# First four output blocks on the unscaled input, with the norm's factor applied at their eviction

## The reference

```python
def rms_norm(x, g):
    y = xf * lax.rsqrt(jnp.mean(xf * xf, axis=-1, keepdims=True) + RMS_EPS)
    return (y * g.astype(jnp.float32)).astype(x.dtype)
...
h = rms_norm(x, g_mix_pre)
proj = jnp.einsum('btd,dc->btc', h, w_in)
q_r, f_r, i_r, g_r, q_a, k_a, v_a = jnp.split(proj, splits, axis=-1)
...
z = heads(f_in)
f = lbh + (1.0 - lbh) * jax.nn.sigmoid(z)
```

## Time and profile before

| | |
|---|---|
| median of 3 runs | 1590.98 us |
| profiled execution | 1592.15 us, span 1590.4 |
| PE busy | 1536.7 us, 97% |
| DVE busy | 997.5 us, 63% |
| ACT busy | 850.3 us, 53% |
| POOL busy | 129.9 us, 8% |
| mean granted clock of PE | 0.993 |
| moved from and to HBM | 156 GB/s over the span |

### The profile page before, as it was taken

The page is one execution under the profiler, slowest core; times in us unless marked ns, Lnnn a source line. Parts: engine busy times, 40 slices in busy tenths (PEclk is TensorE's granted clock), DMA queues, the critical chain, the costliest instruction groups (busy, mean ns, idle before and its releaser), DMA issues.

```text
span 1590.4 us, 29827 instructions
## 1 busy us (share of the span) xinstructions
PE 1536.7 (97%) x11984; PEld 1463.5 (92%) x11984; DVE 997.5 (63%) x1675; ACT 850.3 (53%) x1540; POOL 129.9 (8%) x165
## 2 busy tenths in 40 slices
PE   5999999899999999999999999998999999999996
PEld 5998789898999999999999987898899999999996
DVE  6683778774548655345887656878645675553466
ACT  6445655476455755234664565445755465551552
POOL 4120123000000000000002100330000000000000
PEclk9999999999999999999999999999999999999998
DMA  6644664353454555334443467343534545552453
GB/s 202 202 137 164 235 217 133 107 179 107 134 165 153 167 190 180 114 107 150 155 146 120 141 219 266 121 141 115 169 104 148 164 154 179 182 183 80 133 154 118
DMA packets 83237, 247.89 MB, mean 156 GB/s; under 512 B 8691, under 2 KB 26483, under 8 KB 82972
## 3 DMA queue, kind: packets, MB, share of 16 engines
q1 hardware_dynamic: 83100, 245.98, 48.2%
HBM read 234.13 MB, written 14.44 MB: 156 GB/s over the span
## 4 chain that ended last, share of the span: by engine, by line
PE 86%; DVE 8%; ACT 2%; issue 2%; DMA 1%; SPq 0%; DVEq 0%; ACTq 0%
PE ps L1030 68%; PE ps L1027 7%; PE ps L1083 3%; DVE w_rest L1347 2%; PE ps L1233 1%; PE ps L1220 1%; PE ps L1248 1%; DVE reg L1385 1%; DMA kc<-kcT 1%; DVE x L1389 1%; DVE norm_every L1370 1%; DVE square_sum L1360 1%; ACT w_high L749 1%; PE ps L1058 1%; PE ps L1206 0%
## 5 line engine op out<-in xcount | busy, mean ns | idle before, releaser
L1030 PE MATMUL ps<-h_high,w_rest 128*128 128x320 f32 (+1 forms) x1920 | 581.2, 303 | 8.5 <-DVE h_rest L1409 5.8
L1030 PE MATMUL ps<-h_rest,w_high 128*128 128x320 f32 (+1 forms) x1920 | 570.5, 297 | 0.0
L1030 PE MATMUL ps<-h_high,w_high 128*128 128x320 f32 (+1 forms) x1920 | 570.2, 297 | 0.0
L749 ACT ACTIVATE w_high<-w_raw 128x1024 fp32r<-128x1024 f32 x384 | 402.1, 1051 | 231.4 <-PE ps L1030 231.4
L1347 DVE TENSOR_TENSOR w_rest<-w_raw,w_high 128x1024 fp32r<-128x1024 f32 x380 | 473.0, 1250 | 74.7 <-ACT w_high L749 74.6
L1030 PEld LDWEIGHTS ps<-h_high,w_rest 128*128 128x128 f32 x1920 | 366.4, 191 | 26.1 <-issue 21.6
L1030 PEld LDWEIGHTS ps<-h_rest,w_high 128*128 128x128 f32 x1920 | 366.6, 191 | 0.8 <-issue 0.4
L1030 PEld LDWEIGHTS ps<-h_high,w_high 128*128 128x128 f32 x1920 | 366.5, 191 | 0.0
L1030 PE MATMUL ps<-u_high,w_rest 128*128 128x320 f32 (+1 forms) x1024 | 306.0, 299 | 2.8 <-DVE u_rest L1451 2.4
L1030 PE MATMUL ps<-u_high,w_high 128*128 128x320 f32 (+1 forms) x1024 | 303.8, 297 | 0.0
L1030 PE MATMUL ps<-u_rest,w_high 128*128 128x320 f32 (+1 forms) x1024 | 303.7, 297 | 0.0
(11 more groups left out here) (181 smaller groups left out, 1600.0 us busy)
## 6 DMA issues: line engine op xcount, KB each, us to landing
w_raw<-w SPq DMA_DIRECT2D x384, 512.0 KB, 3.6
kc<-kcT SPq DMA_DIRECT2D x16, 512.0 KB, 8.7
vc<-vc SPq DMA_DIRECT2D x16, 512.0 KB, 7.1
s_in<-s SPq DMA_DIRECT2D x8, 512.0 KB, 5.9
ss<-s_in SPq DMA_DIRECT2D x8, 512.0 KB, 5.9
bias<-rel_scratch SPq DMA_DIRECT2D x8, 512.0 KB, 4.5
rel_scratch<-rel_row SPq DMA_DIRECT2D x1, 2560.0 KB, 12.3
bias<-rel_scratch SPq DMA_DIRECT2D x8, 256.0 KB, 5.4
```

The source lines that it names most:

```text
L749: A.activation(whi[:, v % RING], raw[:, v % RING], ACT.Copy).then_inc(S["w_hi"], 1)
L1030: last = pe.matmul(ps[:, bank, 0:n], wt[:, slot, c, :], xt[:, c, :], **flags)
```

## The change

1. **A copy of the input without the factor.** `first_high` and `first_rest` hold x times gain, split. ACT makes the high part with the gain as scale (`x_high`), DVE the rest (`x_low`), chunk by chunk as x lands. Blocks 0 to 3 (`N_FIRST`) run on these. Block 0 waits for the chunks, block 4 is now the first to wait for `h_high` and `h_rest`.
2. **The factor at the eviction.** DVE multiplies the bank of each of these four by `norm_every` into `tmp` (`f_scaled`), and ACT's two sigmoids read `tmp` in place of PSUM.
3. **Banks.** Blocks 0 to 5 go to banks 0, 1, 3, 4, 2, 7 (`FIRST_BANKS`), so none of them waits for another's eviction.
4. **The norm's place.** The squares follow the high parts of x and of weights 0 and 1 on ACT; the sum over the partitions follows block 1 on PE (`first_sum`), the reciprocal follows the two small operations on `lb` on DVE. The scaled chunks go to a tile of their own, `first_x`.
5. **Weights.** Load 0 is sent first, ahead of x, and the parameters third. DVE makes the rest of load 0, POOL those of 1 to 3. Loads 4 and 5 (`N_SOON`) are split between the norm's steps: their high parts on ACT in front of the first and second pair of chunks, their rests on DVE behind the second and behind the last step of `pre`. From load 6 on the old rule holds: the rest is made in the turn after the freeing block's.

The diff, cut to its core:

```diff
+FIRST_BANKS = (0, 1, 3, 4, 2, 7)
+N_FIRST = 4
+N_SOON = 2
...
         if o.i == 1:
+            here.insert(0, ("first_sum", 0))
             here.append(("rel", 0))
...
+    first_h = place("first_high", [P, KC, WIDE[0]], F32R, offset=part(0, 8))
+    first_l = place("first_rest", [P, KC, WIDE[0]], F32R, offset=part(1, 0))
+    first_x = place("first_x", [P, KC, WIDE[0]], offset=part(1, 10))
...
+            load(0)
             for c in range(0, KC, 2):
                 sp.dma_start(x[:, c:c + 2, 0:WIDE[0]], xT[:, c:c + 2, 0:WIDE[0]]).then_inc(S[f"x_part{c // 2}"], 16)
-            sp.dma_start(prm[:], par).then_inc(S["p_in"], 16)
-            for v in range(RING):
+                if c == 0:
+                    sp.dma_start(prm[:], par).then_inc(S["p_in"], 16)
+            for v in range(1, RING):
                 load(v)
...
-            rest(0)
+            for v in range(1, RING):
+                rest(v)
             for c in range(1, KC, 2):
                 pool.wait_ge(S["h_hi"], c + 1)
...
                 if o.kind == "F":
+                    if o.n < N_FIRST:
+                        act.wait_ge(S["f_mul"], o.n + 1)
+                        src = tmp[:, o.n, 0:n]
...
+            def x_high(p):
+                gain = prm[:, 0, 0:KC]
+                act.wait_ge(S[f"x_part{p}"], 16)
+                for c in (2 * p, 2 * p + 1):
+                    A.activation(first_h[:, c, :], x[:, c, 0:WIDE[0]], ACT.Copy, scale=gain[:, c:c + 1]).then_inc(S["x_hi"], 1)
+
             act.wait_ge(S["one_set"], 2)
+            act.wait_ge(S["p_in"], 16)
+            x_high(0)
+            high(0)
+            for p in range(1, 4):
+                x_high(p)
+            high(1)
             for p in range(4):
                 x_sq(0, 0, p)
-            high(0)
-            norm_sum(0, 0, 0)
-            high(1)
-            for p in range(4):
-                pre(0, 0, 0, p)
             high(2)
             high(3)
+            norm_sum(0, 0, 0)
             act.wait_ge(S["lb_set"], 2)
             A.activation(lb[:], lb[:], ACT.Exp).then_inc(S["lb_exp"], 1)
+            for p in range(4):
+                if p < N_SOON:
+                    act.wait_ge(S["blk"], p + 1)
+                    high(RING + p)
+                pre(0, 0, 0, p)
...
-                    if v + RING < n_loads:
+                    if N_SOON <= v < n_loads - RING:
...
-                hi, lo = (uh[h], ul[h]) if o.kind == "D" else (hh[h], hl[h])
+                hi, lo = (first_h, first_l) if o.n < N_FIRST else (uh[h], ul[h]) if o.kind == "D" else (hh[h], hl[h])
...
             def normed(o, c):
-                k = 0 if o.kind == "F" else 2
+                if o.n == 0:
+                    pe.wait_ge(S["x_lo"], c + 1)
+                    return
...
+            def f_scaled(o):
+                dve.wait_ge(S["blk"], o.n + 1)
+                V.tensor_tensor(tmp[:, o.n, 0:WIDE[0]], ps[:, bank_of(o), 0:WIDE[0]], every[:, 0:WIDE[0]], ALU.mult)\
+                    .then_inc(S["f_mul"], 1)
...
+                elif o.n in (2, 3):
+                    f_scaled(o)
...
+            def x_low(c):
+                dve.wait_ge(S["x_hi"], c + 1)
+                V.scalar_tensor_tensor(first_l[:, c, :], x[:, c, 0:WIDE[0]], prm[:, 0, c:c + 1], first_h[:, c, :].bitcast(F32),
+                                       ALU.mult, ALU.subtract).then_inc(S["x_lo"], 1)
+
+            x_low(0)
+            x_low(1)
+            dve.wait_ge(S["w_hi"], 1)
+            V.tensor_tensor(wlo[:, 0], raw[:, 0], whi[:, 0].bitcast(F32), ALU.subtract).then_inc(S["w_lo_0"], 1)
+            for c in range(2, KC):
+                x_low(c)
             for p in range(4):
                 x_sq(0, 0, p)
-            norm_sum(0, 0, 0)
-            for p in range(5):
-                pre(0, 0, 0, p)
...
+            norm_sum(0, 0, 0)
+            dve.wait_ge(S["n_inv"], 1)
+            for o in outs[:2]:
+                f_scaled(o)
+            for p in range(5):
+                pre(0, 0, 0, p)
+                if p in (1, 4):
+                    rest(RING + p // 4)
...
-                late = [v + RING for v in free_at[o.n] if v + RING < n_loads]
+                late = [v + RING for v in free_at[o.n] if N_SOON <= v < n_loads - RING]
```

More of the change, by code:

```diff
@@ L272, in norm_no, with bank_of @@
     return 2 + 8 * l + {1: 0, 2: 1, 3: 4}[k] + (1 if k == 3 and l == DEPTH - 1 else 2) * h
+def bank_of(o):
+    return FIRST_BANKS[o.n] if o.n < len(FIRST_BANKS) else o.n % GEMM_BANKS
 def rel_buckets(dist):
@@ L448, in build @@
     free_at = {}
-    lo_of = {v: ("w_lo_p", v + 1) for v in range(RING)}
+    lo_of = {v: ("w_lo_p", v) if v else ("w_lo_0", 1) for v in range(RING)}
     for o in outs:
@@ L731, in a_spr @@
                                 ALU.subtract).then_inc(S["a_lo"], 1)
-            rest(0)
+            for v in range(1, RING):
+                rest(v)
             for c in range(1, KC, 2):
                 pool.wait_ge(S["h_hi"], c + 1)
-                V.tensor_tensor(hl[0][:, c, :], acc[0][:, c, :], hh[0][:, c, :].bitcast(F32), ALU.subtract).then_inc(S["h_odd"], 1)
-            for v in range(1, RING):
-                rest(v)
+                V.tensor_tensor(hl[0][:, c, :], first_x[:, c, :], hh[0][:, c, :].bitcast(F32), ALU.subtract).then_inc(S["h_odd"], 1)
             table = {"lev": lev, "wide": wide, "s_upd": s_upd, "kc_own": kc_own, "r_spr": r_spr, "a_spr": a_spr}
@@ L759, in x_sq @@
             def x_sq(l, h, p):
-                if h == 0:
-                    act.wait_ge(S[f"x_part{p}"], 16)
-                elif p == 0:
+                if h and p == 0:
                     act.wait_ge(S["x_in1"], 16)
@@ L790, in pre @@
                     act.wait_ge(S["nap"], 8 * m + c + 1)
-                    A.activation(hh[h][:, c, :], acc[h][:, c, :], ACT.Copy).then_inc(S["h_hi"], 1)
+                    A.activation(hh[h][:, c, :], (acc[h] if m else first_x)[:, c, :], ACT.Copy).then_inc(S["h_hi"], 1)
             uses = [None, None]
@@ L820, in evict @@
                     dst = (vt if o.kind == "I" else va)[o.h]
-                    A.activation(dst[0:rows, o.tile, 256 * o.k:256 * o.k + 256], ps[0:rows, o.n % GEMM_BANKS, 0:256],
+                    A.activation(dst[0:rows, o.tile, 256 * o.k:256 * o.k + 256], ps[0:rows, bank_of(o), 0:256],
                                  ACT.Copy).then_inc(S["ev_a"], 1)
@@ L1329, in a_spr, with first_sum @@
                     held[5 + i] = (S["a_scaled"], 8 * l + 4 * h + 2 * g + i + 1)
-            pe.wait_ge(S["one_set"], 2)
-            norm_sum(0, 0, 0)
-            table = {"norm_sum": norm_sum, "rel": rel, "lev": lev, "k_t": k_t, "v_t": v_t, "upd": upd, "out": out,
+            def first_sum(l):
+                pe.wait_ge(S["one_set"], 2)
+                norm_sum(0, 0, 0)
+            table = {"first_sum": first_sum, "norm_sum": norm_sum, "rel": rel, "lev": lev, "k_t": k_t, "v_t": v_t, "upd": upd, "out": out,
                      "s_rd": s_rd, "s_o": s_o, "s_upd": s_upd, "r_sum": r_sum, "r_spr": r_spr, "sc": sc_, "pt": pt_, "pv": pv,
```

25 lines of the change are left out of this document (14 added, 11 removed).

## The result

Eleven runs of the changed kernel, between eleven of the kernel before on the same chip, have a median of 1595.15 us (1593.24 to 1598.83) against 1592.18 (1590.57 to 1594.62); the ratio is 1.0019, 95% interval 1.0011 to 1.0026. By its interval it is slower by 3 us (0.2%), which is less than the 0.3% (4.8 us) that the prediction took as the least change to be told apart. The profiled execution took 1595.15 us, its span is 1593.3 (before 1590.4) and its mean granted clock 0.990 (before 0.993).

What follows compares the result with a forecast made beforehand. Block 6's start, set by DVE's work behind a late norm, was taken to bound the change: 1.3 us later start plus 1.9 for the lower clock, 3.2 us, on the median 1590.98 gives 1594.2; range 1590.0 to 1597.5.

Steps and rivals of the forecast that it cites:

- Part 1: Kernel start: parameters land at 6.0 us, PE starts at about 10.5 and ends block 1 by 20.5, 7 us ahead.
- Part 2: Norm comes late: the first add waits for POOL until 15.6; DVE's reciprocal can start at 23.3 us, before at 12.84.
- Part 3: DVE from reciprocal to block 6: rest of block 5 ready at 36.4, of block 6 at 45.9, starting 1.3 us later.
- The idle: PE before block 6: stands idle from 40.1 us, for 5.8 us, waiting for DVE's rest of the weights.
- Part 4: Clock at block 6: after the idle it begins at the 1.2 GHz level, losing 1.9 us, bounds 0 and 3.9.
- The sum: Block 6's later start plus its lower clock: 1.3 + 1.9 = 3.2 us later.
- one amount from 60 us on: Sign in the profile after: from 60 us on every PE start is shifted by one amount, about 3 us.
- The rival of the lead that holds: Blocks 0 to 3 onward: if DVE cleared its work early enough, PE stays 7.6 us ahead, 1583.4; chance 0.05.
- The drain of the table loads: ACT's three table loads: each costs its 1.28 us once more, 3.2 + 3.8 = 7.0 us later, 1598.0; chance 0.03.

Runs made afterwards that it cites:

- c_after_split: The changed kernel with the position table's transfer issued in four parts at turns 4 to 7 and nothing else; median 1595.77 us, 1.0017 of the kernel before.
- n_norm: The changed kernel with load 1's rest on DVE ahead of the adds of squares and the root ahead of the fourth w_high on ACT; 1593.74 us.
- e1_slope: The changed kernel with the rest of weight load 6 made twice on DVE, the first time into a dead tile; median 1595.9 us.
- e2_warm: The changed kernel with 18 matmuls on a constant tile in TensorE's wait before block 6; median 1596.09 us.
- n_best: The changed kernel with six edits: load 1's rest on DVE, loads 6 to 9 sooner, scalings ahead, four more banks, table's transfer at turn 3; 1593.75 us.

## Why the prediction was right

The forecast was 1594.2 us in 1590.0 to 1597.5, the measured median 1595.15. Of the 0.95 us between them, 1.2 are the base: the forecast stood on 1590.98, the median of three runs of the kernel before, and eleven gave 1592.18. The change itself cost 2.97 us by the medians, against the 3.2 of the sum.

One control makes the sizes below easier to judge. c_after_split has the same instructions as the changed kernel up to 52 us, so it is a second execution of that stretch: block 6 starts at 45.27 after an idle of 5.70, and ends at 50.99.

```profile
45.27 0.64 PE L1057 MATMUL ps<-h_high,w_rest 128*128 128x320 f32 x1 [5.70 <-DVE w_rest L1383]
```

```profile
50.99 0.44 ACT L827 ACTIVATE tmp<-ps 128x320 f32<-128x320 f32 x1 [1.28 <-PE ps L1057]
```

- **Part 1** held. Parameters at 5.70 (forecast 6.0), high part of block 1 done at 12.6 (13.0), first matmul at 10.27 (10.5), block 0 ended at 15.3 (forecast 17.0 at the half rate; the low rate lasted only 3.1 us).
- **Part 2** held in its mechanism: the first add stands behind GpSimd's subtraction (13.37 and 2.21 us, to 15.58; POOL ends at 15.24), and n_norm takes that away. The reciprocal started at 22.68, forecast 23.3 (its terms add up to 23.2), since the parameters landed 0.3 us sooner and the copies were a little cheaper.
- **Part 3** held. The rest of block 5 was ready at 35.9 (36.4), that of block 6 at 45.4 (45.9), both 0.5 early by part 2's error. From the reciprocal to the rest of block 5 it took 13.2 us (forecast 13.1), from there to that of block 6 9.5 (9.5). Block 6 started 0.8 us later than before, not 1.3. e1_slope puts 1.14 us more into DVE's queue and block 6 starts 1.0 later; n_norm starts the reciprocal 1.48 sooner and block 6 starts 1.26 sooner.
- **The idle** was mis-sized in this execution: 4.6 us, forecast 5.8. The rests came 0.5 earlier, and block 5 ended at 40.8 instead of 40.1, since PE ran at the low rate from 33.7 to 37.2, behind two gaps of 1.13 and 0.81 us. I had priced no clock for short gaps. In c_after_split, with the same gaps and no low rate behind them, the idle is 5.70.
- **Part 4**: right mechanism; the term of 1.9 us was mis-sized for this execution. Block 6 took 6.30 us (45.42 to 51.72) in place of 3.52, so the clock cost 2.8, forecast 1.9. The stretch was 5.5 us, longer than those of the earlier trace rows. In c_after_split block 6 took 5.72 us, so the clock cost 2.2 behind the longer idle. e2_warm shows the term at the place, 2.6 us.
- **The sum**: 0.8 + 2.8 = 3.6 at block 6, forecast 1.3 + 1.9 = 3.2. The two errors have opposite signs, so part of the agreement is luck. c_after_split gives 0.6 + 2.2 = 2.8 at the same place (its block 6 ends 2.81 us later than before), so the forecast lies between two executions, and the size of the clock's term can't be had closer than about 1 us from the rows. The shift was 3.5 at 128.8, 2.6 at 1173.4, and 2.9 in the span; it isn't one amount from 60 us on, as I had said. The clock's later stretches differ: 0.89, 0.89, 0.77 in the windows at 310, 775 and 1090 before, 0.77, 1.00, 0.89 after. By the estimate above that is 1.7 us in favour of the changed kernel, where the shift fell by 0.9, so the windows give the direction and not the size.
- **The rival of the lead that holds** rested on DVE alone. n_best showed that even with DVE cleared a second transfer would have taken it; that was in the trace before the change (rel_scratch, 50.68 to 63) and the prediction has no word of it. It did not enter the number, since DVE took the lead first.
- **The drain of the table loads** did not appear: the load at 5.70 ends at 6.98 and its copy starts at 6.99, the one at 20.82 at 22.10 and its root at 22.12. The Trainium skill (ScalarE: Activation LUTs, What ACT_TABLE_LOAD costs) has the load right at 1283 ns; its further 1380 ns don't show on these switches.
